# Delta masks and level 1 reordered, x loaded first, expert activations and loads issued earlier

## The reference, cut to what matters

```python
# first block
h = h + hybrid_mixer(rmsnorm(h))         # differential attention with rope, and a 31-tap conv branch
h = h + cross_attention(rmsnorm(h), rmsnorm(mem))
h = h + conv_ffn(rmsnorm(h))             # up 2 x 2816 wide, 3-tap conv, silu gate, down
x = rmsnorm(h)
# second block
h = rms_norm(x)
q, k, v, gdn_qkv, z, b, a, gate_sb, gate_gdn = split(h @ w_in)
y_sb  = stick_breaking_attention(q, k, v) @ w_branch_sb
y_gdn = (rms_norm(gated_delta_rule(silu(conv(gdn_qkv)), g, beta)) * silu(z)) @ w_branch_gdn
x = x + (sigmoid(gate_sb) * y_sb + sigmoid(gate_gdn) * y_gdn) @ w_out
# 16384 experts, 16 chosen for each of 8 heads by product keys
x = x + (gates * gelu(rms_norm(x) @ u.T)) @ v     # gates are zero but for the chosen ones
```

## Time and profile before

| | |
|---|---|
| median of 3 runs | 3319.24 us (3318.76 to 3329.38) |
| profiled execution | 3317.98 us, span 3315.7 us |
| granted TensorE clock, mean | 0.995 |
| TensorE busy | 3227.7 us, 97% |
| VectorE busy | 2195.3 us, 66% |
| ScalarE busy | 773.8 us, 23% |
| GpSimd busy | 1834.9 us, 55% |

### The profile page before, as it was taken

The page is one execution under the profiler, slowest core; times in us unless marked ns, Lnnn a source line. Parts: engine busy times, 40 slices in busy tenths (PEclk is TensorE's granted clock), DMA queues, the critical chain, the costliest instruction groups (busy, mean ns, idle before and its releaser), DMA issues.

```text
span 3315.7 us, 40252 instructions
## 1 busy us (share of the span) xinstructions
PE 3227.7 (97%) x15737; PEld 2680.6 (81%) x15737; DVE 2195.3 (66%) x3316; ACT 773.8 (23%) x1248; POOL 1834.9 (55%) x994
## 2 busy tenths in 40 slices
PE   6999999999999999999999999999999999999999
PEld 5787778887877887888888888888878887888887
DVE  6975389963336257564755888788854337888884
ACT  2152322211224122333121111255531011111110
POOL 4547367766541653012666666633356666777775
PEclk9999999999999999999999999999999999999999
DMA  3223122322320221000333444455553336556662
GB/s 132 84 64 102 53 92 97 96 96 89 111 73 26 94 78 58 14 20 31 119 106 117 140 140 138 134 200 207 204 185 105 123 121 208 186 190 200 199 194 99
DMA packets 164525, 391.67 MB, mean 118 GB/s; under 512 B 10865, under 2 KB 69489, under 8 KB 162289
## 3 DMA queue, kind: packets, MB, share of 16 engines
q1 hardware_dynamic: 73408, 262.70, 24.0%
q10 hardware_dynamic: 90928, 126.39, 11.3%
HBM read 326.14 MB, written 62.91 MB: 117 GB/s over the span
## 4 chain that ended last, share of the span: by engine, by line
PE 84%; DVE 11%; issue 2%; ACT 1%; DMA 1%; POOL 0%; DVEq 0%; ACTq 0%; POOLq 0%
PE banks L1519 22%; PE banks L1521 22%; PE banks L1520 22%; PE banks L909 3%; DVE sb_sq L2226 3%; PE banks L802 1%; PE banks L794 1%; PE banks L378 1%; DVE sb_tmp L2236 1%; DVE sb_sq L2224 1%; PE banks L1581 1%; PE banks L1555 1%; PE banks L1557 1%; PE banks L1556 1%; DVE sb_zL L546 1%
## 5 line engine op out<-in xcount | busy, mean ns | idle before, releaser
L1507 POOL TENSOR_TENSOR sb_wL<-sb_raw,sb_wH 128x1024 fp32r<-128x1024 f32 x495 | 1207.5, 2439 | 1454.1 <-PE banks L1521 1401.8
L1519 PE MATMUL banks<-sb_hH,sb_wH 128*128 128x512 f32 x2040 | 820.0, 402 | 12.9 <-ACT sb_sq L1124 3.1
L1520 PE MATMUL banks<-sb_hL,sb_wH 128*128 128x512 f32 x2040 | 796.7, 391 | 0.0
L1521 PE MATMUL banks<-sb_hH,sb_wL 128*128 128x512 f32 x2040 | 796.6, 390 | 0.0
L1502 POOL TENSOR_SCALAR sb_wH<-sb_raw 128x1024 fp32r<-128x1024 f32 x495 | 643.0, 1299 | 14.9 <-DMA sb_raw<-in_weights 14.9
L1519 PEld LDWEIGHTS banks<-sb_hH,sb_wH 128*128 128x128 f32 x2040 | 384.9, 189 | 97.6 <-issue 12.6
L1521 PEld LDWEIGHTS banks<-sb_hH,sb_wL 128*128 128x128 f32 x2040 | 383.8, 188 | 81.3
L1520 PEld LDWEIGHTS banks<-sb_hL,sb_wH 128*128 128x128 f32 x2040 | 385.0, 189 | 73.2 <-issue 1.7
L1519 PE MATMUL banks<-sb_pzH,sb_wH 128*128 128x512 f32 x1024 | 399.8, 390 | 5.9 <-DVE sb_xT L1471 3.8
L1521 PE MATMUL banks<-sb_pzH,sb_wL 128*128 128x512 f32 x1024 | 398.9, 390 | 0.0
L1520 PE MATMUL banks<-sb_pzL,sb_wH 128*128 128x512 f32 x1024 | 398.9, 390 | 0.0
(11 more groups left out here) (432 smaller groups left out, 4623.6 us busy)
## 6 DMA issues: line engine op xcount, KB each, us to landing
sb_raw<-in_weights SPq DMA_DIRECT2D x495, 512.0 KB, 3.7
gates<-sb_stage ACTq DMA_DIRECT2D x16, 2048.0 KB, 7.8
acts<-sb_sq ACTq DMA_DIRECT2D x96, 256.0 KB, 2.0
sb_Gt<-gates ACTq DMA_DIRECT2D x24, 1024.0 KB, 7.5
sb_Ga<-acts ACTq DMA_DIRECT2D x24, 1024.0 KB, 11.1
sb_Gt<-gates ACTq DMA_DIRECT2D x4, 2048.0 KB, 9.8
sb_xT<-in_xT SPq DMA_DIRECT2D x4, 512.0 KB, 9.9
acts<-sb_xT ACTq DMA_DIRECT2D x1, 2048.0 KB, 7.8
```

The lines of the kernel that those rows point to most:

```text
L1507: nc.gpsimd.tensor_tensor(wL[:, t % LOS, :], raw[:, t % RAWS, :], wH[:, t % HIS, :].bitcast(F32), ALU.subtract).then_inc(sems("weights_lo" ...
L1519: pe.matmul(out, hi, H, start=start, stop=False)
L1520: pe.matmul(out, hi, L, start=False, stop=False)
L1521: return pe.matmul(out, lo, H, start=False, stop=stop)
```

## The change

In level 1 of the delta rule each group's update follows its product. The masks of group 1 in the first chunk are made before the chunk loop, and that chunk's values product of group 0 comes after LT. x is loaded first, from both queues, with the constants behind its first piece; all eight squares are added by VectorE and summed once; the lambda parameters are worked after the norm. ScalarE's first two activations of the late experts come before its wait for the stored gates, `sq` is used four deep in the late groups, and the first half loads of the early v stage are issued in the last late group.

```diff
@@ -816,7 +816,9 @@
                 for lv in range(1, LEVELS):
                     for c in range(2):
                         off_blocks(lv, c)
-                    for c in range(2):
+                        if lv == 1:
+                            updates(1, c)
+                    for c in range(2 if lv > 1 else 0):
                         updates(lv, c)
                     if lv == 1:
                         emptied(E, TILE["z"] + 2 * tb)
@@ -1107,46 +1109,62 @@
...
+            t0 += 8 * EARLY
+
+            def late_gelu(n, t):
+
+                tile_ready(E, t)
+                E.at("pz_v", n - 3)
+                act.activation(sq[:, n % 4, :], bank(t), ACT.Gelu).then_inc(sems(f"bank_free{BANK[t]}"), 1)
+
+            for b in range(4):
+                E.eng.wait_ge(sems(f"spilled{b}"), 16 * 2 * EARLY)
+            late_gelu(0, t0)
+            late_gelu(1, t0 + 1)
             for jj in range(2):
                 E.eng.wait_ge(sems(f"stage_out{jj}"), 16 * (TG // 2))
-            for b in range(4):
-                E.eng.wait_ge(sems(f"spilled{b}"), 16 * 2 * EARLY)
             E.meet()
-            t0 += 8 * EARLY
             by_group = gates.rearrange("g p (n e) t -> n p g (e t)", e=8)
+            gh = gates.rearrange("g p (n f e) t -> n f p g (e t)", f=2, e=4)
+            ah = acts.rearrange("(n f e) p t -> n f p e t", f=2, e=4)
+
+            def load_gates(i, f):
+
+                E.eng.wait_ge(sems("pz_v"), 8 * (LATE + i - 1) + 4 * f + 4)
+                eng.dma_start(B["Gt"][:, :, 4 * f:4 * f + 4, :].rearrange("p g e t -> p g (e t)"), gh[i, f]).then_inc(sems(f"half_in{f}"), 16)
+
+            def load_acts(i, f):
+
+                E.eng.wait_ge(sems("pz_v"), 8 * (LATE + i - 1) + (4 * f + 4 if i else 0))
+                eng.dma_start(B["Ga"][:, 4 * f:4 * f + 4, :], ah[i, f]).then_inc(sems(f"half_in{f}"), 16)
+
             for g in range(LATE):
                 E.at("pz_v", 8 * g)
                 eng.dma_start(B["Gt"][:].rearrange("p g e t -> p g (e t)"), by_group[g + EARLY]).then_inc(sems("gates_in"), 16)
                 for e in range(8):
                     n = 8 * g + e
-                    tile_ready(E, t0 + e)
-                    E.at("pz_v", n - 1)
-                    act.activation(sq[:, e % 2, :], bank(t0 + e), ACT.Gelu).then_inc(sems(f"bank_free{BANK[t0 + e]}"), 1)
+                    if n > 1:
+                        late_gelu(n, t0 + e)
                     if e >= 1:
                         E.at("pz_v", n)
                         act.activation(B["pzH"][:, 0, e - 1, :], tmp[:, (e - 1) % 4, :], ACT.Copy).then_inc(sems("pz_hi"), 1)
+                    if g == LATE - 1 and e in (1, 2):
+                        load_acts(0, e - 1)
+                    elif g == LATE - 1 and e == 5:
+                        load_gates(0, 0)
                 E.eng.wait_ge(sems("pz_v"), 8 * g + 8)
                 act.activation(B["pzH"][:, 0, 7, :], tmp[:, 3, :], ACT.Copy).then_inc(sems("pz_hi"), 1)
...
-            gh = gates.rearrange("g p (n f e) t -> n f p g (e t)", f=2, e=4)
-            ah = acts.rearrange("(n f e) p t -> n f p e t", f=2, e=4)
-
-            def load_half(i, f):
-
-                E.eng.wait_ge(sems("pz_v"), 8 * (LATE + i - 1) + 4 * f + 4)
-                eng.dma_start(B["Gt"][:, :, 4 * f:4 * f + 4, :].rearrange("p g e t -> p g (e t)"), gh[i, f]).then_inc(sems(f"half_in{f}"), 16)
-                eng.dma_start(B["Ga"][:, 4 * f:4 * f + 4, :], ah[i, f]).then_inc(sems(f"half_in{f}"), 16)
-
-            load_half(0, 0)
-            load_half(0, 1)
+            load_gates(0, 1)
             for i in range(EARLY):
                 for e in range(8):
                     E.eng.wait_ge(sems("pz_v"), 8 * (LATE + i) + e + 1)
                     act.activation(B["pzH"][:, (i + 1) % 2, e, :], tmp[:, e % 4, :], ACT.Copy).then_inc(sems("pz_hi"), 1)
                     if i + 1 < EARLY and e % 4 == 3:
-                        load_half(i + 1, e // 4)
+                        load_gates(i + 1, e // 4)
+                        load_acts(i + 1, e // 4)
...
@@ -1263,6 +1281,7 @@
                         chain(ins)
                 empties(ins, t)
...
+            decay_blocks(0, 1)
             for tb in range(TB):
                 ts = slice(tb * P, (tb + 1) * P)
...
@@ -1279,12 +1298,16 @@
                     v.tensor_scalar(g["X"], g["X"], 0.0, None, ALU.min).then_inc(sems("gd_dT"), 1)
                     E.wait("gd_turned")
                     v.tensor_tensor(g["kw"], bank4(0), gs(6, c), ALU.mult).then_inc(sems("gd_kw"), 1)
-                    v.tensor_tensor(g["vb"], bank4(1), gs(0, c), ALU.mult).then_inc(sems("gd_vb"), 1)
+                    values = lambda: v.tensor_tensor(g["vb"], bank4(1), gs(0, c), ALU.mult).then_inc(sems("gd_vb"), 1)
+                    if tb or c:
+                        values()
                     v.tensor_tensor(g["er"], g["er"], B["gq"][:, h, ts], ALU.mult)
                     E.wait("gd_dTe")
                     E.eng.wait_ge(sems("gd_rows"), 2 * (2 * tb + c) + 2)
                     chain(v.tensor_tensor(g["LT"], g["X"], bank4(5), ALU.mult))
-                    if c == 0:
+                    if tb == c == 0:
+                        values()
+                    if c == 0 and tb:
                         decay_blocks(tb, 1)
                     E.wait("gd_kk")
                     chain(v.tensor_tensor(g["aT"], bank4(3), g["X"], ALU.mult))
@@ -1437,7 +1460,7 @@
                     if e < 8:
                         emptied(E, t0 + e)
                         E.at("pz_ready", n - 3 if e >= 4 else 8 * g)
-                        v.tensor_tensor(by_tg(tmp[:, e % 4, :]), by_tg(sq[:, e % 2, :]), B["Gt"][:, :, e, :],
+                        v.tensor_tensor(by_tg(tmp[:, e % 4, :]), by_tg(sq[:, e % 4, :]), B["Gt"][:, :, e, :],
                                         ALU.mult).then_inc(sems("pz_v"), 1)
...
@@ -1483,8 +1506,9 @@
         @block.sync
         def _(sp):
             x_blocks = a["xT"].rearrange("(n k p) t -> n p k t", p=P, k=2)
-            for n in range(KB // 2):
-                sp.dma_start(xT[:, 2 * n:2 * n + 2, :], x_blocks[n]).then_inc(sems(f"x_in{n}"), 16)
+            sp.dma_start(xT[:, 0:2, :], x_blocks[0]).then_inc(sems("x_in0"), 16)
+            sp.dma_start(cst[:], a["consts"]).then_inc(sems("consts_in"), 16)
+            sp.dma_start(xT[:, 4:6, :], x_blocks[2]).then_inc(sems("x_in2"), 16)
...
@@ -1586,7 +1610,13 @@
 
             if first:
 
-                sum_added(E)
+                E.made("norm")
+                E.n["made sq"] = KB
+                pe.wait_ge(sems("sq_used"), KB)
+                for t in range(TB):
+                    mm = pe.matmul(ps[2][:, t:t + 1], dg[:, 0, t * P:(t + 1) * P], ones[:, 0:1], start=(t == 0), stop=True,
+                                   skip_group_check=True)
+                mm.then_inc(sems("both_sums"), 1)
                 spread_pe(E)
 
                 def memory_norm(b, k):
@@ -1821,13 +1851,12 @@
         @block.scalar
         def _(eng):
             E = side(eng, "act")
-            eng.dma_start(cst[:], a["consts"]).then_inc(sems("consts_in"), 16)
+            x_blocks = a["xT"].rearrange("(n k p) t -> n p k t", p=P, k=2)
+            eng.dma_start(xT[:, 2:4, :], x_blocks[1]).then_inc(sems("x_in1"), 16)
+            eng.dma_start(xT[:, 6:8, :], x_blocks[3]).then_inc(sems("x_in3"), 16)
             eng.dma_start(par[:], a["params"][:, 0:N_KEPT]).then_inc(sems("consts_in"), 16)
-            if first:
-                eng.dma_start(tmp[:, 3, 0:256], a["params"][:, N_KEPT:N_PARAM]).then_inc(sems("lam_in"), 16)
-            if first:
-                eng.dma_start(B["pos"][:], a["pos"].partition_broadcast(P)).then_inc(sems("pos_in"), 16)
-            eng.wait_ge(sems("consts_in"), 32)
+            eng.dma_start(B["attT"][:, 1, 0:256], a["params"][:, N_KEPT:N_PARAM]).then_inc(sems("lam_in"), 16)
+            eng.dma_start(B["pos"][:], a["pos"].partition_broadcast(P)).then_inc(sems("pos_in"), 16)
 
             def copy_tiles(name, n, to, w=S, at=0, func=ACT.Copy):
                 for b in range(n):
@@ -1843,11 +1872,10 @@
 
             if first:
 
-                E.wait("lam_sums", 2)
-                act.activation(sc[:, 2:4], sc[:, 0:2], ACT.Exp).then_inc(sems("lam_exp"), 1)
+                act.preload_act_table(ACT.Sqrt)
                 for k in range(KB):
                     eng.wait_ge(sems(f"x_in{k // 2}"), 16)
-                    square(E, xT[:, k, :], ready="sq_early" if k < KB - 1 else "sq_ready")
+                    square(E, xT[:, k, :], ready="sq_early")
                 root_act(E, TB)
                 for k in range(KB):
                     hi_part(E, hH[:, k, :])
@@ -1857,6 +1885,8 @@
                 E.wait("angles")
                 act.activation(B["sin"][:], B["att"][:, 0, :], ACT.Sin).then_inc(sems("sines"), 1)
                 act.activation(B["cos"][:], B["att"][:, 0, :], ACT.Sin, scale=0.5).then_inc(sems("sines"), 1)
```

(25 more changed lines are left out.)

## The result

The changed kernel takes 3302.91 us (median of 7 runs, 3299.57 to 3308.83) against 3319.24 (7 runs beside them, 3317.53 to 3329.75): ratio 0.9947, 95% interval 0.9937 to 0.9957, so it is faster by 0.5%. That is inside the range and 8 us over the point forecast; it lies outside the 3290 to 3299 to which the prediction gave a chance of 0.55. The profiled execution took 3303.71, with a span of 3301.5, 14.2 less than before.

What follows compares the result with a forecast made beforehand. TensorE, busy 97% of the span, was taken to set the pace. The terms 6.5 + 5.2 + 7.6 + 5.5 - 0.9 = 23.9 us off the profiled 3317.98 gave 3294.1, forecast as median 3295, range 3288 to 3304.

Steps and rivals of the forecast that it cites:

- the point forecast: Whole kernel: a median of 3295 us, with 3290 to 3299 as its own range at chance 0.55.
- the best ends: Upper gains of the five places: 7.3, 5.4, 7.9, 5.6 and +0.7, given as summing to 3288.5 us.
- Start: Loading of x and squares: last addition at 16.5, first product near 25; gain 6.5 us, between 7.3 and 3.3.
- My 17.0 and 19.7: Start: end of VectorE's last addition if it waits for GpSimd's short first pass, or falls behind the long one.
- The second rival: Start: x lands no earlier than 14.5, or last additions fall behind GpSimd's long pass; 3.2 us less, 3298; chance 0.14.
- Masks: Delta, first chunk: masks ahead and values later remove waits and keep group 1's grams at full clock; gain 5.2 us.
- Level 1: Delta, four chunks: next level starts 4.1 us after S, group 1's product start, instead of mean 6.01; gain 7.6.
- about 1 per chunk is left: Level 1: if the new three-part gap still pulls the clock down, about 1 us per chunk remains, 4 in all.
- The first rival: Delta: the clock stays down at masks and level 1; 1.9 and 3.6 us less, 3300.5; chance 0.18.
- Early to late: Early to late experts: the stall moves two tiles later, to the third activation, about 4.2 us; the place costs 0.9.
- Late to early: Late to early groups: earlier loads remove TensorE's 3.78 us wait and the slow tile; gain 5.5 us.
- The slower rival: Up-projections: multiply-adds meet GpSimd in a worse phase; from mean 1.92 us the gain is lost, at 2.0 3326; chance 0.03.

Runs made afterwards that it cites:

- Experiment 3: The changed kernel with GpSimd's first pass held until VectorE's last addition of squares: 3302.92 us (0.9941 of the kernel before).
- experiment 6: The kernel before with only the first chunk's group 1 masks made ahead and its first values product moved behind LT: 3315.26 us (0.9983).
- Experiment 4: The changed kernel with GpSimd's low pass behind each chunk's second z tile held until level 2's last masks product: 3295.77 us (0.9923).
- experiment 8: The changed kernel with both GpSimd holds (start, level 1) and the third and fourth late activations before the first rounding copy: 3284.59 us (0.9895).
- experiment 9: As experiment 8, with the constants issued behind the third piece of x instead of ahead of it: 3281.50 us (0.9884).
- experiment 1: The changed kernel with the first two late activations put back behind the waits for the stored gates: 3303.75 us (0.9948), run again 3302.39.
- Experiment 2: The changed kernel with the third and fourth late activations issued ahead of the first rounding copy: 3297.13 us (0.9932).
- experiment 5: The kernel before with only the new order of level 1, each group's update behind its product: 3313.29 us (0.9974).
- experiment 7: The kernel before with only the loads of the first early half moved up into the last late group: 3313.56 us (0.9978).

## Why the prediction was right, and where it was off

The kernel got faster at three places as the sum has it, and at the fourth, level 1, through the clock and not through the order. Its time is inside the range. The sum is 9.6 us too large against the profiled executions. The range's lower end was wrongly added up: the best ends make 26.9 us, which is 3292.4 on the scale of the forecast, not 3288.5.

**Start: the term was mis-sized, by 3.8.** The order of x worked: landing, squares and one set of sums are as forecast, and the 6.57 from variance to first product is unchanged. (The last piece of x before was issued at 2.24 and landed at 14.03, not at 2.7 and 14.5; that changes little.) What failed is when GpSimd starts. "GpSimd starts at 15.4 in either order, since the same bytes stand ahead of the first weight tile" failed. The same bytes are issued ahead, but not all of them land ahead: the lambda parameters and the positions land at 13.7 and 15.7, beside the weights, whose first tile is there by 13.65. Before, both had landed by 11.7 and the first weight tile at 15.3. My 17.0 and 19.7 were the right cases; 18.29 lies between them, because GpSimd came into the middle of the four. Experiment 3 shows it: with GpSimd held, 15.56 and 24.25, better than the 15.9 and 25.0 forecast. The second rival had this mechanism with 3.2 us less; 1.9 of it came true at the first product. The rest was lost behind the first product. Of that about 1.2 is chance: in four of the five other profiles of the same start, the end of tile 0 was 4.7 to 4.8 ahead and weight tile 24 3.8 to 4.1 (in the fifth 4.3 and 3.2). In the profile of before the products at 158.33 ran at full pace, while in the other twelve those behind this wait ran at half pace for a time, with a mean clock of 0.66 to 0.72 over the five microseconds from the wait's end.

The Trainium skill (SBUF — State Buffer, Who interferes with whom) says that a VectorE instruction with two SBUF inputs contends with a GpSimd one that reads SBUF, and calls the port pair that they share an exclusive lock. The trace agrees: the last two additions end 0.54 and 0.55 behind the passes that they meet, the four take 5.68 against 3.08, and the R of level 0 takes 2.24 against 0.69.

**Masks: right.** 5.4 against 5.2; the waits of 0.59 and 1.01 are those that I gave as 0.6 and 1.25.

**Level 1: size 1.9 too large, and the mechanism half wrong.** The prediction has the next level start at S + 4.1 because group 0's update fills the gap before S, with the clock as a part of it. But the old order takes 4.18 from S at full clock too (experiment 6), and TensorE's waits are 11.6 us against 13.3. The order gained by cutting the wait of 3 us into pieces, behind which the clock stayed up more often; that rests on the counts in experiment 6 (17 of 28 against 1 of 12). So "about 1 per chunk is left" at half pace is not borne out: such chunks took 5.0 to 6.3 (mean 5.6) in the new order and 5.5 to 7.0 (mean 5.9) in the old, and the mean gain from S over all profiles is 1.0 a chunk, 4.0 in all, not 7.6. That the profiled execution gained 5.7 here is luck in part: three of its four chunks kept the clock, against 17 of 28. The account of its 1.9: S to the next level is 4.17 to 4.18 at full clock (forecast 4.1): 0.3 in four chunks. In the first chunk S stands 5.11 behind the tile, not 4.71, 0.4 less. "S itself doesn't move" took for fixed what GpSimd's pass sets (2.75 us long at 1294.93, 2.35 before). In the second chunk the clock fell behind these short breaks, 0.9, and 0.3 more in its next level (2.33 for sixteen products, not 2.02). The first rival held for one chunk of four here, and for 11 of 28 over all profiles; its "every break over 3 us did so" failed once, in experiment 6. Experiment 4 shows that the 5.11 were GpSimd's, so more was to be had than I forecast: with GpSimd held, all twelve chunks of experiments 4, 8 and 9 took 4.07 or 4.08 from S.

**Early to late: the step that failed by most, 4.2.** The stall is two tiles late and stands at the third activation, as written, but is 6.98 long and not 4.2. Shifted by the 13.8 us that the kernel was ahead there, my wait was to last from 2436.3 to 2440.55; it lasted from 2436.2 to 2443.19. The store took 1.8 longer and the load 1.3, of which a shorter way from landing to activation gave 0.45 back: I took both durations from a trace in which TensorE, and with it the weight loads, stood still beside them. With TensorE stopped early the store took 7.2 again in both profiles of experiment 1, and the load 11.1 and 10.9. That it is the weight loads that slow them is argued, not shown, though the profiles go with it: in the six in which TensorE stopped beside the store, 0.23 to 0.29 MB of weights moved during it and it took 7.24 or 7.25; in the other seven it was 0.51 to 0.54 MB and 8.5 to 9.1. Experiment 2 is one of these, with a store of 8.9 and a load of 11.1. The rest, 1.4, is the longer stretch at half pace (8.6 for the tile, not 7.2). What I missed most is that the four-deep buffer does allow a better order, worth 10 us (experiment 2); I had it as not helping "since the order on ScalarE is the same", which is true of this change alone.

**Late to early: right.** 5.55 against 5.5, and 5.55 alone. The cost that I gave ScalarE for the issues was not there: 0.37 each and not 2.8.

**The slower rival** didn't come: the multiply-adds of the up-projection had a mean of 1.69 us, under the 1.92 from which it would have decided, and the offset of the tiles doesn't change there.

**The point forecast.** The profile of before was a good execution: over 27 runs of it beside experiments 5 to 8 the median is 3321.0, 3 over the profiled 3318.0. Of thirteen profiles nine lost about 1.6 us at one of two places, the products near 237 or near 815, where before, after and two others didn't. The sum took the luck of one execution as the rule.

## What to carry to other kernels

A wait that moves is not yet a wait that is gone: write down the order of the engine that releases it, instruction by instruction, and look for the one that stands behind a transfer; here the order decided 10 us, and the change had moved only half of what it could. Where a helper engine's passes aren't wanted soon, let them wait for the few operations of the critical chain that they lengthen; two such waits were worth 2.7 us at the first product and 7 us on the median. Durations of transfers taken from a stretch in which the main engine stood still were too short for one in which it ran. And before a new order of instructions is credited with a gain, compare both orders at the same clock: here they took the same 4.18 us, and what the new one changed was how often the clock stayed up.

## What the runs showed of the hardware

**The clock behind short waits is not the same in every execution.** The windows at one place, of the changed kernel and of experiment 1, whose instructions are the same there (busy time of PE, PEld, DVE, ACT, POOL, then granted clock, DMA share, GB/s):

```profile
810.00:815.00 5.00, 5.00 (x29) 4.37 (x30) 2.61 (x16) 0.99 (x3) 2.59 (x2) 1.00 0.34 108
```

```profile
810.00:815.00 5.00, 5.00 (x18) 4.00 (x18) 3.59 (x19) 0.35 (x2) 1.53 (x2) 0.66 0.31 108
...
1531.00:1536.00 5.00, 5.00 (x18) 4.36 (x18) 0.00 (x0) 1.83 (x5) 0.00 (x0) 0.54 0.00 0
1536.00:1541.00 5.00, 5.00 (x18) 4.24 (x17) 0.00 (x0) 1.20 (x1) 0.00 (x0) 0.50 0.00 0
```

A clock of 1.00 is 2.4 GHz and 0.50 is 1.2. The stretch at 1531 followed waits of 0.26 and 0.90 us; the changed kernel had the same two waits and stayed at 1.00. So waits far under 3 us can cost 1.5 to 5 us, in some executions. Nor does a longer wait always cost: behind the 3.04 us of experiment 6 the clock stayed at 1.00. The Trainium skill (TensorE: Matmul & The Clock Gate, Part 1) says that the number of products at the lower clock at a kernel's start changed from run to run of one kernel; these traces show such changes behind waits in its middle.

**Issuing a large load from ScalarE is cheap when no other issue stands right before it.** The load of the activations took 5.52 us as the last of four issues in a row, 2.6 to 4.4 us right behind the issue of the gates in 22 places of the changed kernel, and 0.37 in the two where it stood alone.
